# Two stages without gathers, regrouped by token tile, and scan products on half the columns

## The reference, cut to what matters

```python
def token_mixer(h, w_in_l, w_out_l, conv_w_l, lbf, lbb, s0f, s0b, conv_fn):
    iv, zf, zb, q, g, cg, bg, hv = jnp.split(h @ w_in_l, SPLITS, axis=-1)
    o_rec, s_f, s_b = hgrn2_mix(q, iv, zf, zb, g, lbf, lbb, s0f, s0b)   # gated linear attention, both ways
    o_conv = bg * conv_fn(cg * hv, conv_w_l)
    y = jnp.concatenate([o_rec, o_conv], axis=-1) @ w_out_l
    return y, s_f, s_b

def peer_ffn(h, wq, subkeys, u, v):                  # 8 heads, 16 experts each, of 16384
    qr = (h @ wq).reshape(bsz, t, PEER_HEADS, 2, PEER_HALF)
    scores = jnp.einsum('bthpd,hpkd->bthpk', qr, subkeys)
    s1, i1 = lax.top_k(scores[..., 0, :], PEER_TOPK)
    s2, i2 = lax.top_k(scores[..., 1, :], PEER_TOPK)
    ...                                              # top 16 of the 256 sums, softmax gate
    act = jax.nn.gelu(jnp.einsum('ted,td->te', u[ek], hk), approximate=False)
    return jnp.einsum('te,ted->td', gk * act, v[ek])

# per layer l: ctx then x
x = x + g1 * token_mixer(modulate(rms_norm(x, n1), sh1, sc1), ...)
x = x + g2 * peer_ffn(modulate(rms_norm(x, n2), sh2, sc2), ...)
```

## Time and profile before

| | us |
|---|---|
| median of 3 runs | 4150.15 (4144.27 to 4165.97) |
| the profiled execution's time | 4162.62 |
| its span | 4160.8 |
| PE busy | 2609.5 (63%) |
| DVE busy | 2879.5 (69%) |
| ACT busy | 661.9 (16%) |
| POOL busy | 927.9 (22%) |
| chain that ended last: PE, DVE, DMA, issue | 34%, 28%, 28%, 9% |

### The profile page before, as it was taken

How to read it: one execution, slowest core, us unless ns; L and a number is a source line. 1 busy time by engine, 2 the same in 40 slices (tenths; PEclk the granted TensorE clock), 3 DMA queues, 4 the chain that set the end, 5 groups by cost and what they waited for, 6 DMA issues and landing times.

```text
span 4160.8 us, 30360 instructions
## 1 busy us (share of the span) xinstructions
PE 2609.5 (63%) x10018; PEld 1562.1 (38%) x10018; DVE 2879.5 (69%) x5590; ACT 661.9 (16%) x1096; POOL 927.9 (22%) x794
## 2 busy tenths in 40 slices
PE   7886997765786650007966664666420185987598
PEld 2855574431111110005724441111210163967396
DVE  2646788699885588886876379855889753546354
ACT  1211201111000010001002111000000142533053
POOL 0001233322323333442330022333344200000000
PEclk9998999886898765558967885688665597998899
DMA  7346898987999989998993287898999631445144
GB/s 252 112 152 237 318 363 331 379 327 280 403 393 369 400 323 382 374 372 313 374 369 134 86 314 276 316 370 344 399 377 385 237 125 42 176 156 198 42 167 150
DMA packets 277108, 1156.45 MB, mean 278 GB/s; under 512 B 19128, under 2 KB 19769, under 8 KB 178217
## 3 DMA queue, kind: packets, MB, share of 16 engines
q0 software_dynamic: 112784, 812.45, 50.2%
q1 hardware_dynamic: 162584, 336.37, 22.4%
q10 hardware_dynamic: 1600, 5.96, 0.4%
HBM read 1150.57 MB, written 4.13 MB: 278 GB/s over the span
## 4 chain that ended last, share of the span: by engine, by line
PE 34%; DVE 28%; DMA 28%; issue 9%; ACT 1%; SPq 0%; POOL 0%; POOLq 0%; DVEq 0%; ACTq 0%; PEldq 0%
DMA arena<-in_peer_uv,arena 17%; DMA ring<-in_w_mod 8%; DVE arena L2158 6%; PE ps L725 4%; PE ps L726 4%; PE ps L727 4%; DVE arena L2134 4%; PE ps L1058 4%; PE ps L833 3%; PE ps L951 3%; PE ps L710 2%; PE ps L1014 2%; DVE w_lo L1705 1%; PE ps L819 1%; DVE arena L2008 1%
## 5 line engine op out<-in xcount | busy, mean ns | idle before, releaser
L2419 POOL DMA_INDIRECT arena<-in_peer_uv,arena x768 | 914.0, 1190 | 2348.0 <-DVE arena L2158 1038.6
L1058 PE MATMUL ps<-arena 128*128 128x512 f32 x1072 | 674.6, 764 | 748.7 <-DVE arena L2144 748.4
L2134 DVE CUSTOM_DVE_ANT_0 arena<-arena,hA 128x1024 f32<-128x1024 f32 x512 | 625.9, 1223 | 291.3 <-DMA arena<-in_peer_uv,arena 285.6
L1058 PEld LDWEIGHTS ps<-arena 128*128 128x128 f32 x1072 | 227.5, 232 | 1137.3 <-issue 568.0
L2158 DVE SCALAR_TENSOR_TENSOR arena<-arena 128x1024 f32<-128x1024 f32 x493 | 630.9, 1280 | 0.1
L1484 ACT ACTIVATE arena<-arena 128x2 f32<-128x2 f32 x384 | 78.1, 203 | 2427.9 <-DVE arena L2134 2427.9
L2134 DVE CUSTOM_DVE_ANT_0 arena<-arena,hB 128x1024 f32<-128x1024 f32 x256 | 312.6, 1221 | 113.7 <-DMA arena<-in_peer_uv,arena 111.8
L833 PE MATMUL ps<-ring,condS 128*2 128x512 f32 x576 | 295.4, 661 | 139.7 <-DMA ring<-in_w_mod 139.7
L1705 DVE TENSOR_TENSOR w_lo<-ring,w_hi 128x1024 fp32r<-128x1024 f32 x220 | 264.1, 1222 | 161.3 <-ACT w_hi L1302 154.7
L725 PE MATMUL ps<-hT_hi,w_hi 128*128 128x256 f32 x992 | 287.2, 290 | 28.0 <-DVE hT_lo L1713 25.5
L726 PE MATMUL ps<-hT_lo,w_hi 128*128 128x256 f32 x992 | 285.3, 288 | 0.0
(11 more groups left out here) (292 smaller groups left out, 3401.0 us busy)
## 6 DMA issues: line engine op xcount, KB each, us to landing
ring<-in_w_mod SPq DMA_DIRECT2D x48, 2048.0 KB
ring<-in_w_in SPq DMA_DIRECT2D x16, 2048.0 KB
ring<-in_w_mlp_in SPq DMA_DIRECT2D x64, 512.0 KB, 6.3
ring<-in_w_mlp_out SPq DMA_DIRECT2D x64, 512.0 KB, 5.8
ring<-in_peer_wq SPq DMA_DIRECT2D x12, 2048.0 KB
ring<-in_w_in SPq DMA_DIRECT2D x44, 512.0 KB, 5.9
vec<-mods SPq DMA_DIRECT2D x31, 512.0 KB
ring<-in_w_out SPq DMA_DIRECT2D x6, 2048.0 KB
```

The lines of the kernel that those rows point to most:

```text
L1058: mm = pe.matmul(ps[:, 6 + c, :], uv[:, j % SLOTS, 0:P], uv[:, j % SLOTS, D + c * CW:D + (c + 1) * CW], start=start, stop=stop)
L2134: dve.tensor_tensor_reduce(row, row, peer_buf[p][:, t, :], 1.0, 0.0, ALU.mult, ALU.add, dots[:, column(j):column(j) + 1]).then_inc(dot_don ...
L2419: pool.indirect_dma_start(uv[:, j % SLOTS, :], None, A["peer_uv"], at).then_inc(uv_full[j % SLOTS], 16)
```

## The change: tile by tile, and half of each scan product

**Tile by tile.** In both stages attention product, square, mean square, root, weighing, output product, residual, norm, turning, queries and scores are made per tile of 128 tokens (`attend_tile`, `mean_square_tile`, `weigh_tile`, `out_part`, `gated_tile`, `norm_tile`, `first_queries`, `first_scores`). The first pick follows tile 0's scores. Tile 1's residual, norm, queries and scores come behind that pick on DVE and PE. In stage 2 the convolution's half of the output product is issued before the scan's half: for tile 0 before the states, for tile 1 behind the mean squares. The norm rows of `p_c0` and `p_x1` get a place of their own in the gather slots (`alt_rows`), so that gathers 4 and up (in stage 2, 516 and up) wait until both tiles are normed. Tile 0's part of `norm("n_c1")` moves into the last slots of the first weave. ACT loads the root's table ahead. The states' transposes are released to ACT by direction.

**Half products.** In `level`, the forward product is made only for the right half of each block of columns and the backward product only for the left half, 64 columns each, through an access with a step (blocks of 1 column at level 0, 64 at level 6). Both land in one bank, and one mask copies both: two copies a level. In the weave a level takes one step in every second slot.

The diff, cut to its core:

```diff
             def level_pieces(m):
-                times, base = TIMES[m], {1: 9, 3: 25}[m]
-                for i in range(16):
-                            elif i % 2:
-                                mm = pe.matmul(o, KF[:, h, ts], QF[:, h, ts], start=True, stop=True)
-                            else:
-                                mm = pe.matmul(o, KB[:, h, ts], QB[:, h, ts], start=True, stop=True)
...
+            def level(base, i):
+                pe.wait_ge(lev_ready, base + i + 1)
+                for h in range(HEADS):
...
+                            for side, k, q in ((1, KF, QF), (0, KB, QB)):
+                                half = [v.rearrange("p (n two b) -> p n two b", two=2, b=1 << (i - 1))[:, :, side, :]
+                                        for v in (o, q[:, h, ts])]
+                                mm = pe.matmul(half[0], k[:, h, ts], half[1], start=True, stop=True)
+                mm.then_inc(lev_mm, 1)
...
-                self.level = [r + 4 + i for i in range(16)]
+                self.level = [r + 4 + 2 * i for i in range(9)]
...
             def mixer0():    # PE
                 modulation0(8, 9)
                 pe.wait_ge(scan_ready, 1)
-                attend(0, range(HEADS)).then_inc(o_done, 1)
-                mean_square(0, 6)
+                for t in range(NT):
+                    attend_tile(0, t, 4 + t)
+                mean_square_tile(0, 0, 6)
                 modulation0(9, 10)
+                mean_square_tile(1, 1, 7)
                 pe.wait_ge(mix_ready, 1)
-                tokens(L_out[0], mixT)
-                make_states(0, ivN)
+                for c in range(2):
+                    enter(L, c, 0, L.e0 + c)
+                    out_part(0, c, 0, CONV + SCAN, True, True).then_inc(tile_mm, 1)
+                pe.wait_ge(mix_ready, 2)
+                out_part(0, 0, 1, CONV + SCAN, True, True).then_inc(ring_done, 1)
+                turn_tile("p_c0", hA, 0)
+                out_part(0, 1, 1, CONV + SCAN, True, True).then_inc(ring_done, 1)
+                tile_turned("p_c0", 0)
+                first_queries(0, 0)
+                first_scores(0, 0)
+                pe.wait_ge(score_out, 1)
+                make_states(0, ivN)
+                turn_tile("p_c0", hA, 1)
+                tile_turned("p_c0", 1)
+                first_queries(0, 1)
+                first_scores(0, 1)
...
+            for c in range(2):    # PE, stage 2, behind the three input products
+                enter(L_out[3], c, 0, L_out[3].e0 + c)
+                out_part(3, c, 0, CONV, True, False)
             pe.wait_ge(scan_ready, 4)
             make_states(1, ivN1)
-            attend(3, range(HEADS)).then_inc(o_done, 1)
-            mean_square(2, 6)
-            pe.wait_ge(mix_ready, 3)
+            for t in range(NT):
+                attend_tile(3, t, 6 + t)
+            for t in range(NT):
+                mean_square_tile(3 + t, t, 4 + t)
             for c in range(2):
+                out_part(3, c, 1, CONV, True, False)
+            pe.wait_ge(mix_ready, 4)
+            for c in range(2):
+                out_part(3, c, 0, SCAN, False, True).then_inc(tile_mm, 1)
+            pe.wait_ge(mix_ready, 5)
+            for c in range(2):
+                out_part(3, c, 1, SCAN, False, True).then_inc(ring_done, 1)
...
+            def peer_entry(name, gate, p, dst, done):    # DVE
+                L, v = L_out[{0: 0, 2: 3}[p]], alt_rows[name]
+                dve.wait_ge(alt_full, rows_in[name])
+                norm_rows(v)
+                gated_tile(gate, L, dst, hA, 0, done)
+                squares_tile(dst, 0, hA)
+                norm_tile(name, dst, 0, v)
+                run(pick((p, 0, 0)))
+                gated_tile(gate, L, dst, hA, 1, done)
+                squares_tile(dst, 1, hA)
+                norm_tile(name, dst, 1, v)
+                rows_done(name)
...
+            def context_tile():    # DVE, last slots of the first weave
+                yield FIRST_PAIRS - 4
+                dve.wait_ge(vec_full, rows_in["n_c1"])
+                squares_tile(cs, 0, hA)
+                yield FIRST_PAIRS - 3
+                norm_rows(vec)
+                norm_tile("n_c1", cs, 0, vec)
...
+                if j == 4:    # POOL, before gather j
+                    pool.wait_ge(vec_used, stage_no["p_c0"] + 1)
+                    pool.wait_ge(st_done, 1)
+                if j == SEG_END[4] + (-SEG_END[4]) % SLOTS:
+                    pool.wait_ge(vec_used, stage_no["p_x1"] + 1)
```

More of the change, by code:

```diff
@@ new lines, in mean_square_tile, with out_part @@
+            def mean_square_tile(n, t, bank):
+                pe.wait_ge(o_sq, n + 1)
+                pe.matmul(ps[:, bank, :].rearrange("p (h t) -> p h t", h=HEADS), mean_mat[:, :],
+                          OSQ[:, :, t * P:(t + 1) * P], start=True, stop=True).then_inc(o_ms, 1)
+            def out_part(m, c, t, ks, first, last):
+                L = L_out[m]
+                for k in ks:
+                    x = HV[:, k - HEADS] if m == 3 and k >= HEADS else mixT[:, k]
+                    mm = pe.matmul(ps[:, 2 * ((L.e0 + c) % 2) + t, :], x[:, t * P:(t + 1) * P],
+                                   ring[:, (L.g0 + c) % 2, k, :], start=first and k == ks[0], stop=last and k == ks[-1])
+                return mm
@@ new lines, in _, with first_queries @@
+            CONV, SCAN = list(range(HEADS, KT)), list(range(HEADS))
+            def first_queries(p, t):
+                L = L_wq[p]
+                s = enter(L, 0) if t == 0 else L.g0 % 2
+                for b in range(4):
+                    o = ps[:, 2 * (L.e0 % 2) + t, b * P:(b + 1) * P]
+                    for k in range(KT):
+                        mm = pe.matmul(o, ring[:, s, k, b * P:(b + 1) * P], hT[:, k, t * P:(t + 1) * P],
+                                       start=k == 0, stop=k == KT - 1)
+                mm.then_inc(query_mm if t == 0 else ring_done, 1)
@@ L1969, in front_pieces @@
                 weigh_queries(m, base + 1)
-                for i in range(16):
+                for i in range(LEVELS + 1):
                     yield times.level[i] + 1
@@ L2218, in _ @@
             mixer0()
-            norm("p_c0", cs)
-            run(pick((0, 0, 0)))
             weave(0, FIRST_PAIRS, segment, pick_pieces(PICK_ORDER[1:5]), early_mods(),
```

361 lines of the change are left out of this document (246 added, 115 removed).

## The result

The changed kernel takes 4086.64 us against 4152.89 (median of four, 4144.27 to 4165.97): ratio 0.9843, 95% interval 0.9822 to 0.9865, 66 us less. Its 4086.64 is the median of four runs, 4084.75, 4085.95, 4087.33 and a disturbed one of 10328.67, which the ratio leaves out; the median of the three is 4085.95. Six more runs on another chip had a median of 4086.72 (4075.76 to 4094.33), where the kernel before had 4156.36. The profiled execution took 4085.95, that of before 4162.62.

What follows compares the result with a forecast made beforehand. No engine was taken as the bound, but the latency chain of the stages before the gathers. 21.3 + 3.5 + 38 + 1.5 = 64.3 us off the profiled 4162.6 gives 4098.3, or 4086 as median; range 4058 to 4112.

Steps and rivals of the forecast that it cites:

- Stage 1 up to the gather: Stage 1, input product's end to first gather: tile-by-tile order takes 77.9 us instead of 110.2, 32 less.
- The scan part: Scan of stage 1: 14 copies fewer and half products win 3.5 us (0 to 10).
- What comes back in stage 1: Behind stage 1's first pick: DVE waits 11.1 us longer for tile 1's scores, leaving 21.3 net.
- Halves cost what wholes cost: Level products: 64 columns save almost nothing over 128, as the weight load limits; 3.6 us a level.
- Stage 2: Between the weaves, flush to the second weave's first gather: 52.0 us less, 47.0 of it after the scan's end.
- The start: Stage 2's start: tile 0's split and norm move into the weave's last slots, so PE starts 5.0 us earlier.
- What comes back in stage 2: Start of the second weave: tile 1's late part delays added rows, about 14 us lost, 38 net.
- Levels in the weave: Both mixers' levels in the weave: 28 copies fewer and merged slots win 1.5 us in all (0 to 14).
- 1 (halves halve): Level products: 64 columns take half the time, a level 1.9 us; 20 us more gained, 4066; chance 0.13.
- 2 (tile 1 costs more): Tile 1's late queries and next chunk run slow at a lower clock: 10 us more lost per weave, 4106; chance 0.17.
- 3 (the weave catches up): Slack in the weave's slots 1 to 10 returns the 25 us lost behind the picks: 4061; chance 0.12.
- 4 (accesses with a step): Level products with stepped columns run slower; at six times per column 140 us are lost, 4225; chance 0.04.

Runs made afterwards that it cites:

- tile1_first: The changed kernel with tile 1's residual, norm, turning, queries and scores taken ahead of tile 1's late place behind the pick, in both stages: 4067.94 us against 4086.72.
- full_columns: The changed kernel with each level product over all 128 columns instead of 64: 4094.15 us against the changed kernel's 4086.6.
- levels_split: The changed kernel with each level of the weave in two slots again, eight half products in each: 4075.07 us, ratio 0.9827 to the kernel before.
- t1_split: The changed kernel with tile 1 ahead of the pick in both stages and each weave level in two slots: 4052.51 us, ratio 0.9755 to the kernel before.

## Why the prediction held, and where it did not

- **Stage 1 up to the gather, right.** 77.9 forecast from the input product's end, 76.6 measured; first gather forecast near 302, 295.6 to 299.9 measured in the eleven profiles with the new stages. The list on PE without waits is the chain, as said. The terms of the 77.9 as written add up to 77.6. The turning was mis-sized: 1.8 forecast, 1.09 measured. A turning is one entry, not two, and the 16 that the price was read from took 3.65 because the granted clock at their start was 0.50 (297 to 301). The scan part brought 4.8 (3.5 forecast), and 7.1 against the second profile of before.
- **What comes back in stage 1, right.** 11.1 forecast, 10.2 measured (33.1 against 22.9), and tile1_first took exactly that away.
- **Halves cost what wholes cost, right**: a level 3.68 in stage 1 (3.6 forecast), and full_columns shows it. That the weight load is the reason was argued and stays so. The Trainium skill's rule for a weight load (TensorE: Matmul & The Clock Gate, section LDWEIGHTS) pointed the same way.
- **Stage 2, right.** 52.0 forecast, 50.2 measured in the first pair of profiles and 48 to 54 over all with this order. The start won 5.2 (5.0). From the scan's end the chain took 75.8 (72.9). What the prediction had too small were the convolution's first half, which held the states for 4.0 (0.4 forecast) since its weights landed at 2239.0, the wait for the query weights, 3.97 (2.0), and the queries, 9.85 at a granted clock of 0.74 (7.2); the states in turn took 7.1 for 10.3.
- **What comes back in stage 2, right in kind, a little large.** 14 forecast, 10 to 12 measured (141.0, 139.0 to 151.0).
- **Levels in the weave: the wrong step.** The prediction said that the merged slots move no DMA, that PE has no idle and that the copies are worth 1.5. In mixer 1 the stretch grew by 6 to 8, and the DMA rate over it fell from 366 to 353 GB/s. The premise was a window of 50 us in which PE was busy 50.0 of 50; over all of pairs 16 to 40 PE had stood 9.9 for DVE's diagonals in the same profile, and in the changed kernel it stood 14.1. I summed the work of each engine and not who waits for whom within two slots. The earlier trace rows already had the wait (3.9 at the copies), and the diff the doubled step of `times.level`. In mixer 3 the loss and the gain by the copies are of one size and cancel. levels_split and t1_split show what the term could have been: 0 in mixer 1, 4 to 10 in mixer 3.
- **The sum: errors that nearly cancel.** By the stretches of the first two profiles stage 1 brought 38 - 10 = 28 (24.8 forecast, 3 too little), stage 2 50 - 10 = 40 (38, 2 too little), the levels in the weave -7 (+1.5, 8.5 too much). That makes 61 for 64.3; the timed runs say 66, and the rest lies in stretches that scatter. That the median (4086.6) met the forecast of 4086 to the microsecond is luck.
- **Rivals.** 1 (halves halve) falls with full_columns. 2 (tile 1 costs more): the mechanism is there, 64 query entries took 9.16 at a granted clock of 0.80, and 7.41 at 1.00 when PE had paused for no more than 0.79, but the price was 2, not 10. It goes with the clock and not with the load on the DMA: tile 0's entries in stage 1 took 7.38 at a clock of 1.00 beside a DMA share of 0.78. 3 (the weave catches up) falls with tile1_first. 4 (accesses with a step): level 0, every second column, took 3.68 like all others. The Trainium skill's warning (Advanced Engine Details and Errata, section PSUM Cachelines) that any non-contiguous access slows matmuls significantly is not borne out at this size: the six levels with gaps took what the seventh took, whose 64 columns are contiguous. A cost that stays below the 0.115 of an entry would not show.

The two windows behind rival 2, both over 64 query entries of tile 1 in stage 2, of the changed kernel and of tile1_first, in the columns of the earlier trace rows:

```profile
2326.00:2335.00 9.00, 9.00 (x64) 8.93 (x64) 2.47 (x4) 0.00 (x0) 0.71 (x1) 0.80 0.98 410
```

```profile
2273.40:2280.70 7.30, 7.30 (x64) 7.14 (x64) 7.06 (x39) 0.00 (x0) 0.00 (x0) 1.00 0.01 2
```

## What to carry to other kernels

When work leaves a woven schedule, look at the slots and not at the sums: two engines that hand work to each other want their long slots at the same time, and merging two half steps into one step every second slot cost 7 us in mixer 1 although one engine had 9 less to do. When a stage is cut into tiles so that the first can go ahead, put the second tile into the wait that the first one leaves (here 18 us) rather than behind the next step. And one profile is one execution: a stretch at the end of the program differed by 15 us between two of the same kernel, so compare stretch by stretch, and the noisy ones over several profiles.

## What the runs showed of the hardware

- An f32 product with a stationary of 128 x 128 takes nearly the same with 64 moving columns as with 128 (full_columns): 273 and 275 ns an entry in the records, 3.68 and 3.73 us for 32 entries, at a granted clock near 1.00; the weight load beside it is recorded at 192 ns.
- A moving operand and a PSUM target with a step of two f32 values, and with blocks of 2 to 32 values and gaps as long, cost nothing that shows in these products: 3.68 each for all seven levels, the last of which has its 64 columns in one piece.
- The 64 query entries of one tile took 7.41, 9.16 and 9.58 us at mean granted clocks of 1.00, 0.80 and 0.76. Ahead of the second PE had stood for 24.67 us before the turnings and for 0.69 after them, ahead of the third for 4.29.
- The second weave's last 111 pairs took 716 to 731 us in fourteen profiles of kernels that are the same there, and nothing in the study tells what decides it.
